# An eleven-tile expert ring, loaded in order, with x kept in HBM between the norms, in a hybrid decoder layer on one core

## What is computed

```python
x = layer_norm(ALPHA * x + g1 * mix, ln1_g, ln1_b)
hf = modulate(x, sh2, sc2)
ff = hier_moe(hf, ...)   # per token: best of 4 groups, then 2 of its 8 experts
#   expert e: (silu(h @ we_gate[e]) * (h @ we_up[e])) @ we_down[e]
x = layer_norm(ALPHA * x + g2 * ff, ln2_g, ln2_b)
```

## Time and profile before

| | us |
|---|---|
| three timed runs | 1441.33, 1443.5, 1445.74 (median 1443.5) |
| the profiled execution | 1444.49 |
| its span, first to last instruction | 1442.7 |
| mixer, up to the last "pb" job | 0 to 669.4 |
| "wo", norms, routing | 669.4 to 797 |
| expert stage on PE | 800.6 to 1373.3 |
| weighing, last norm, stores | 1373.3 to 1442.7 |

### The profile page before, as it was taken

One profiled execution on the slowest core, in us unless ns is written; L12 is line 12 of the kernel. 1 busy time (PEld: TensorE's weight loads), 2 busy tenths in 40 slices (PEclk: granted clock), 3 DMA queues, 4 the chain that ended last, 5 costly groups with the idle time before them and its releaser, 6 DMA issues.

```text
span 1442.7 us, 17957 instructions
## 1 busy us (share of the span) xinstructions
PE 1184.8 (82%) x6154; PEld 722.5 (50%) x6155; DVE 399.3 (28%) x696; ACT 307.8 (21%) x463; POOL 127.2 (9%) x204
## 2 busy tenths in 40 slices
PE   4899999999999999999882687988877888887700
PEld 3687878546778888886442232333323323333200
DVE  3316270143652100103866111111111111111165
ACT  3346470332122000001000021211111111211121
POOL 0100000000000100000000111111111111111134
PEclk9899999899999999999895798999999989999955
DMA  8744431213452314131026559978999999999531
GB/s 282 240 173 160 176 117 59 79 59 120 151 183 88 117 59 175 59 120 33 16 108 256 189 222 400 360 300 329 386 389 401 396 391 369 400 387 370 235 134 46
DMA packets 70232, 307.86 MB, mean 213 GB/s; under 512 B 10079, under 2 KB 18912, under 8 KB 57221
## 3 DMA queue, kind: packets, MB, share of 16 engines
q1 hardware_dynamic: 59946, 295.29, 53.3%
q0 software_dynamic: 6272, 10.14, 2.2%
q10 hardware_dynamic: 3964, 1.73, 0.5%
HBM read 299.00 MB, written 18.55 MB: 220 GB/s over the span
## 4 chain that ended last, share of the span: by engine, by line
PE 63%; DMA 18%; DVE 9%; issue 4%; ACT 3%; SPq 2%; ACTq 0%; POOL 0%; POOLq 0%; DVEq 0%; PEldq 0%
PE ps L1519 29%; DMA mem<-in_we_up 14%; PE ps L1795 13%; PE ps L1804 6%; PE ps L1629 4%; PE ps L1754 3%; PE ps L1787 2%; DMA mem<-in_w_mod 2%; PE ps L1552 1%; DVE mem L1482 1%; DMA mem<-in_we_gate 1%; DVE mem L1481 1%; PE ps L1736 1%; PE ps L1680 1%; DVE mem L1224 1%
## 5 line engine op out<-in xcount | busy, mean ns | idle before, releaser
L1519 PE MATMUL ps<-mem 128*128 128x260 f32 (+1 forms) x2080 | 465.5, 385 | 10.1 <-ACTq L863 3.9
L1519 PEld LDWEIGHTS ps<-mem 128*128 128x128 f32 (+1 forms) x2080 | 391.0, 189 | 80.8 <-issue 12.2
L1795 PE MATMUL ps<-mem 128*64 128x512 f32 x1120 | 287.2, 672 | 94.3 <-DMA mem<-in_we_up 72.6
L1795 PEld LDWEIGHTS ps<-mem 128*64 128x64 f32 x1120 | 90.0, 154 | 265.5 <-issue 265.5
L1461 DVE TENSOR_TENSOR mem<-mem,ps 64x512 f32<-64x512 f32 x35 | 24.1, 690 | 426.7 <-ACT mem L1028 426.7
L1804 PE MATMUL ps<-mem 128*64 128x512 f32 x560 | 129.6, 605 | 3.4 <-issue 3.4
L1028 ACT ACT_TABLE_LOAD x35 | 44.9, 1283 | 367.4 <-PE ps L1795 367.4
L721 POOL DMA_INDIRECT pair_scratch<-mem x35 | 32.7, 934 | 453.9 <-DVE mem L1453 453.9
L1804 PEld LDWEIGHTS ps<-mem 128*64 128x64 f32 x560 | 37.6, 138 | 67.0 <-issue 64.8
L1453 DVE COPY mem<-ps 64x512 f32<-64x512 f32 x70 | 48.2, 688 | 78.4 <-PE ps L1804 77.3
L1754 PE MATMUL ps<-mem 128*128 128x512 f32 x128 | 59.0, 621 | 0.0
(11 more groups left out here) (290 smaller groups left out, 890.5 us busy)
## 6 DMA issues: line engine op xcount, KB each, us to landing
mem<-in_we_gate SPq DMA_DIRECT2D x32, 2048.0 KB, 11.9
mem<-in_we_up SPq DMA_DIRECT2D x32, 2048.0 KB, 15.9
mem<-in_we_down SPq DMA_DIRECT2D x32, 2048.0 KB, 9.0
mem<-in_w_in SPq DMA_DIRECT2D x14, 2048.0 KB, 8.0
mem<-in_w_mod SPq DMA_DIRECT2D x12, 2048.0 KB, 11.6
out<-mem SPq DMA_DIRECT2D x13, 512.0 KB, 5.2
mem<-in_state_gla SPq DMA_DIRECT2D x8, 512.0 KB, 3.9
mem<-v_scratch SPq DMA_DIRECT2D x8, 512.0 KB, 4.2
```

Source lines behind the costliest of these rows:

```text
L1519: ins = pe.matmul(out[0:m, h, 0:HALF], w[:, k, col:col + m], src[:, k, h * HALF:(h + 1) * HALF], start=(k == 0), stop=(k == KD - 1))
L1795: ins = pe.matmul(ps[CAP * q:CAP * q + CAP, 2 + j, :], xT[j][:, k, :], ring[3 * slot + q][:, k, :], start=(k == 0), stop=(k == KD - 1))
```

## The change

The buffers are laid out anew. The six expert tiles become eleven: `gate_ring` and `up_ring` with four slots each, `down_ring` with three. Expert e takes slot e % 4 and e % 3, every expert is loaded in order, and SP's loop is written out for 28 experts. `plan` now gives PE a slot and a turn for each ring; PE picks the slot with nested branches and waits for that slot's semaphore alone.

To make room, x is not held in SBUF: DVE's LN1 loop reads x from three buffers `xb`, loaded from the input again by `load_x`, and SP stores the new x to `x1_scratch` beside `hf` and loads it back as `x1` after the last expert tile. LN1's rows, the modulation and the first three x tiles are loaded during the mixer by SP; LN2's rows and g2 come with `x1` instead of by POOL.

PE's step is written in another order: gate and up of block b, the turn of block b-1's activation, the turn of block b+1's rows, the down product of block b-1. ACT copies the turned activation of b-1 first and takes the silu of b last.

```diff
-            sp.wait_ge(job_done, INDEX[("gb", 7)] + 1)
-            sp.dma_start(mod_samp[0:NS].rearrange("p v d -> p (v d)"), mod_dram[0:NS, 2 * D:5 * D]).then_inc(mod_back, 16)
...
+            def load_x(p):
+                i = ORDER[p]
+                if p >= 3:
+                    sp.wait_ge(x1_out[p % 3], 16)
...
+            for k, name in enumerate(("ln1_g", "ln1_b")):
+                sp.dma_start(lnp[:, k, :], t[name][0:1, :].to_broadcast([P, D])).then_inc(lnp_in, 16)
+            load_x(1)
+            load_x(2)
...
+            def load_gate_up(e):
+                for to, name in ((gate_ring, "we_gate"), (up_ring, "we_up")):
+                    sp.dma_start(to[e % 4], t[name][0, e].rearrange("(p k) n -> p k n", p=P)).then_inc(gu_in[e % 4], 16)
...
+            sp.wait_ge(job_done, INDEX[("gb", 7)] + 1)
+            load_gate_up(0)
+            sp.wait_ge(z_ready, KD)
+            sp.wait_ge(w_used, len(WTILES) - 2)
+            load_down(0)
...
+            sp.wait_ge(rows_out, 64)
+            load_gate_up(1)
+            store_hf(0)
+            store_hf(1)
+            load_x(3)
+            load_x(4)
+            store_hf(2)
+            store_hf(3)
             sp.wait_ge(job_done, INDEX[("wo", ORDER[4])] + 1)
-            load_expert(0, 0, 0)
-            load_expert(0, 1, 0)
-            load_expert(0, 2, 0)
-            load_expert(1, 0, 1)
+            load_down(1)
+            load_gate_up(2)
             store_hf(4)
...
+            load_down(2)
+            load_gate_up(3)
             sp.wait_ge(blocks_ready, 1)
...
+            for e in range(4, NE):
+                after = sp.value_load(plan[0:1, LD_AFTER + e - 4:LD_AFTER + e - 3], min_val=0, max_val=NBLK)
+                sp.wait_ge(gu_done, after + 2)
+                sp.sem_inc(sp_turns, 1)
+                load_gate_up(e)
+                sp.wait_ge(dn_done, after + 2)
+                sp.sem_inc(sp_turns, 1)
+                load_down(e - 1)
...
+            def block_step(i, j):
...
+                    gate_up_of(i * 2 + j, j)
+                    if not first:
+                        turn_act(1 - j, i + (1 + j), i + j)
+                    pe.wait_ge(xg_in[1 - j], i * 16 + 16 * (1 + j))
+                    pe.wait_ge(xT_ready[1 - j], i + (1 + j))
+                    transpose_rows(1 - j)
+                    if not first:
+                        finish(i, j)
```

More of the change, by code:

```diff
@@ L195, in build @@
         K2 = area(Z0 + 2080, HEADS, NT)
+        xn = [area(TB + 1024 * j, D) for j in range(2)]
+        packrows = area(TB + 2048, D)
         EX = area(TB, HEADS, NT)
@@ L311, in build @@
         iota_i = rtmp(64)
[L315 to L325, removed]
+        place_oh = rtmp(2 * TILES, CAP)
+        block_oh = rtmp(2 * TILES, NBLK)
+        named = rtmp(2 * TILES * NBLK * 2).rearrange("p (n b c) -> p n b c", b=NBLK, c=2)
+        assert TB + 3968 >= rt[0] - 2080
         job_done = sem("job_done")
@@ L426, in build @@
         pe_turns = sem("pe_turns")
+        act_turns = sem("act_turns")
         pool_turns = sem("pool_turns")
@@ L740, in _ @@
             two_blocks(0)
-            with pool.Fori(1, NBLK // 2) as i:
+            two_blocks(1)
+            with pool.Fori(2, NBLK // 2) as i:
                 two_blocks(i)
-            for j in range(2):
-                pool.wait_ge(moved[j], 16)
+            pool.wait_ge(tail_in, 16 * 6)
             for p, i in enumerate(ORDER):
@@ new lines, in block_step @@
+            def block_step(i, j):
+                first = isinstance(i, int) and j == 0
+                with sc.If(n > i * 2 + j):
+                    if not first:
+                        copy_acT(1 - j, i + (1 + j), i * 2 + j)
+                    sc.wait_ge(xt_done[1 - j], i + (2 + j))
+                    sc.wait_ge(gu_done, i * 2 + (j + 2))
+                    sc.activation(xT[1 - j], ps[:, 1 - j, :].rearrange("p (k n) -> p k n", k=KD), ACT.Copy)\
+                      .then_inc(xT_ready[1 - j], 1)
+                    sc.wait_ge(gu_done, i * 2 + (j + 3))
+                    sc.wait_ge(act_ready[j], i + 1)
+                    sc.activation(sg[j][CAP:2 * CAP, :], ps[0:CAP, 2 + j, :], ACT.Silu).then_inc(sg_ready[j], 1)
+                if not first:
+                    with sc.Else():
+                        with sc.If(n > i * 2 + (j - 1)):
+                            copy_acT(1 - j, i + (1 + j), i * 2 + j)
+                        sc.sem_inc(act_turns, 1)
@@ L1038, in weigh @@
+            for j in range(2):
+                block_step(0, j)
+            with sc.Fori(1, NBLK // 2) as i:
+                for j in range(2):
+                    block_step(i, j)
             def weigh(i):
@@ L1777, in _ @@
             out = start(("plan", 0))
-            for k in range(5):
+            for k in range(4):
                 ins = pe.matmul(out[0:1, 0, k * NBLK:(k + 1) * NBLK], plan_f[:, k:k + 1], ident[:, 0:NBLK],
@@ L1869 @@
+            for j in range(2):
+                block_step(0, j)
+            with pe.Fori(1, NBLK // 2) as i:
+                for j in range(2):
+                    block_step(i, j)
 _INS = ["x_prompt", "x_sample", "state_conv", "state_rglru", "state_gla", "c_prompt", "c_sample", "w_mod", "b_mod",
```

416 lines of the change are left out of this document (218 added, 198 removed).

## The result

| | us |
|---|---|
| before, median of 4 runs | 1443.01 (1441.33 to 1445.74) |
| changed, median of 4 runs | 1373.41 (1371.09 to 1377.09) |
| ratio | 0.951, interval 0.949 to 0.954 |
| the profiled execution of the changed kernel | 1377.09, span 1375.3 |
| the changed kernel again (experiment 12), median of 5 | 1373.97, ratio 0.953 (0.951 to 0.954) |

The time is 69.6 us lower. The forecast was 1382, with a range of 1365 to 1412: the side and the range held, and the forecast was 8.6 us too high. In the profiled executions PE's last down product ends at 1306.11 where it ended at 1373.33; 1311.6 was forecast. What follows it takes 69.2 us, before 69.4.

The account below looks back on a forecast made before the run. Expert tile transfers were taken to bound the late stage. An earlier start, shorter steps and 16.5 us batches end PE at 1311.6, 61.7 us less, with the tail unchanged: 1444.49 - 61.7 = 1382.8, forecast 1382, range 1365 to 1412.

Parts of the forecast that it names:

- What bounds the stage: Late expert stage bound by expert tile transfer, DMA share 0.97; the stage before leaves the same engines idle, share 0.13.
- The prefetch: Before the first block: eleven expert tiles issued instead of five, 60 us of transfer, ended by some 781, costing nothing.
- The batch: Expert stage: one expert's down, gate and up tiles take 16.5 us; bounds 16.3 and 16.75; twenty batches, 330 us.
- When the queue becomes full: Expert stage: SP's queue idles 10 us before expert 1's end and 7 us before expert 7's, then never empties.
- The step: PE's block step: 12.31 us of products plus 0.2 and 0.7 us of gaps, 13.2 in sum; bounds 12.3 and 14.8.
- The start: Before the expert stage: 4.7 us saved, so the first gate and up product starts at 800.2; bounds 0 and 5.5.
- The working for the first norm's rows: LN1: rows loaded during the mixer let DVE start 3.3 to 3.5 us earlier; 3.5 us counted.
- The last part: From the last gate and up product's start to the last down product's end: 22.8 us, as before the change.
- No shorter step: Rival, chance 0.15: branches and waits keep PE's step at 15.3 us, PE sets the pace, time 1418.
- Fetched again: Rival, chance 0.09 (slower): PE's longer loop is fetched every step, up to 5.7 us each; step 18.9, time 1540.
- Late prefetch: Rival, chance 0.05: waits on SP leave six of eleven tiles, 33 us, for the expert stage; time 1415.

Follow-up runs that it names:

- experiment 12: The changed kernel again, unchanged, as base on the third chip; 1373.97 us, ratio 0.953.
- Experiment 4: Changed kernel loading only half of each expert tile from expert 4 on (down: from expert 3), all engine instructions kept; 1314.07 us.
- experiments 3 and 10: Changed kernel with a smaller ring: 3 has six tiles (two slots of each kind), 1421.22 us; 10 has nine (three slots each), 1387.82 us.
- Experiment 1: Changed kernel with the old order of a block's step on PE and ACT, ring and start kept; 1370.17 us, ratio 0.950.
- experiment 9: Changed kernel with six tiles (two slots each) and the old order of a step on PE and ACT; 1420.96 us, ratio 0.984.
- experiment 7: Changed kernel with the first norm's two rows loaded late again, by ACT's queue behind the last mixer product; 1379.40 us, ratio 0.956.
- experiment 2: Changed kernel with six of the eleven early expert tiles issued only behind the first gathers; 1380.39 us, ratio 0.956.
- experiment 5: Changed kernel with 512 further matrix instructions in PE's block loop, behind a branch never taken; 1373.30 us, ratio 0.952.

## Why the prediction was right, and where its sizes were off

**What bounds the stage: right.** It said that transfers bound the stage, and that the engines stand idle ahead of it while tiles could move. The prefetch came as worked out: the last six tiles are issued from 746.69 and 767.48 (745 and 764 were forecast), and the DMA share from 669 to 790 is 0.51 (near 0.5); only the gate and up of expert 0 came earlier, at 642. Experiment 4 shows the first (60 us gone with half the load), experiments 3 and 10 the second: nine instead of six tiles give 33.4 us, eleven instead of nine 13.9, together 47.2 of the 68. Not all of that is transfer moved ahead. Of the 33.4 us some 14 are the pace, an estimate from 16.65 - 15.96 = 0.69 us for each of the last 20 experts; for the pace the forecast gave depth almost nothing (16.65 to 16.5).

**The batch: right in the mean, wrong in both halves.** 16.5 us were taken for each of the twenty batches behind expert 7. From its end at 954.29, where SP issues the next down tile, to the gate and up product of expert 31 at 1286.31 they take 332.0/20 = 16.6. But this is no constant, and that the mean fits is luck: the forecast let the queue run empty ahead of 958, while at 954 earlier tiles were still queued, and the later batches ran below its bound. The ten batches from 856.42 to 1030.72 take 17.4 us each, and the sixteen experts from there on 15.97. The queues (packets, MB, share of 16 engines' time) from 856 to 1030, then from 1031 to 1286:

```profile
q1 hardware_dynamic: 4427, 64.59, 92.8%
q0 software_dynamic: 2240, 4.27, 7.2%
...
q1 hardware_dynamic: 7271, 102.89, 97.5%
q0 software_dynamic: 2560, 2.78, 3.4%
```

q0 is POOL's gathers and scatters: early they take 7.2% of the engines' time, late 3.4%, since PE's steps of 12.22 us bring them more often and the experts with two blocks have fuller ones (4.27 MB for 14 blocks, 2.78 for 16). What is left to the tiles is 371 GB/s early and 404 late; by the shares 404 would become 404 x 92.8/97.5 = 385, so q0 explains 19 of these 33 GB/s, and the other 14 stay open. And 64.59 MB are 1.7 more than ten batches of 6.29: some tiles issued later had moved before the one that PE waited for had landed.

The forecast had 16.3 us as the least for a batch in a queue that never runs empty, got by scaling a share of 0.97 to 0.99. The measured 15.97 is below it. The scaling holds and the 0.99 does not: the share is 1.01 from 880 to 900 in the kernel before and 1.01 from 860 on in the changed one, and 16.65 x 0.97/1.01 = 15.99. Two rows of the DMA view from 1100 to 1200, GB/s in 40 slices and an expert tile's size and median landing, show where the share was missing. Before:

```profile
GB/s 321 415 442 401 421 419 321 419 423 431 429 426 347 360 429 369 379 433 413 341 334 418 400 438 419 301 367 397 426 365 382 433 295 433 413 418 362 433 347 13
...
mem<-in_we_up SPq DMA_DIRECT2D x6, 2048.0 KB, 16.7
```

And after:

```profile
GB/s 410 390 439 426 426 423 359 382 419 433 439 433 420 338 397 419 433 433 415 446 421 426 426 433 418 393 362 426 419 433 426 439 380 341 439 426 426 410 433 423
...
mem<-in_we_down SPq DMA_DIRECT2D x6, 2048.0 KB, 39.1
```

Before, the last tile of a batch lands 16.7 us after it is issued, and batches are 16.65 us apart: each is issued as the one before runs out, and the rate falls to 350 GB/s or less in nine of the forty slices, to 13 in the last. After, a tile spends 39 us in the queue, with two further batches behind it, and only two slices lie so low. That the pace hangs on the depth is shown by experiments 3 and 10 (16.65 with two slots, 15.96 with three); that it is lost at the handover is read from these rows, and no run took it apart.

**When the queue becomes full: right in kind.** Two idle stretches were forecast, 10 us ahead of expert 1's end and 7 us ahead of that of expert 7. The share of 0.54 from 800 to 860 is the first, and larger; the second did not come, since the share is 1.01 from 860 on, and expert 7 ends at 954.3 where 958.2 was worked out with the longer step.

**The step: forecast 13.2, measured 12.22, and nearly without effect.** The 0.7 us that were left open ahead of the gate and up product are none. One cost was missed, 3.28 us marked issue at 838.75, where PE enters the loop. Experiment 1, with the old order in the same ring, has 0.41 us there, and experiment 3, with the new order and six tiles, none; why is open. The larger miss is one of attribution: the text names the order as what shortens the step, and in experiment 1 the old order has 12.77 us. Its sum gave the step ten times its length's change; between 12.22 and 12.77 that would be 5.5 us, and experiments 1 and 9 show none of it. How long a step may become before the end moves was not tried.

**The start: forecast 800.2, measured 801.62**, and 799.05 in experiment 12. The working for the first norm's rows was 3.5 us; experiment 7 measures 5.4, since in the changed kernel the late loads also meet an expert tile.

**The last part: 22.8 us taken over from before, 19.8 measured.** Its last wait is 1.16 us instead of 2.92, and its last down product 3.67 instead of 5.37; neither the value loads nor PE's clock was counted there. The clock's share is not the change's: the same product takes 5.37 us in experiments 2 and 4. So the 5.5 us by which PE's end was forecast too late are 3.9 of expert 7's earlier end and 3.0 of the last part, less 1.4 of the batches (332.0 us to the last gate and up product where 330.6 were worked out). Of the 8.6 us in all, the other 3 are the profiled execution's distance to the median: 3.7, where 1 was assumed.

**The rivals.** *No shorter step* did not happen. *Fetched again* did not either, by the queue's own rows. *Late prefetch* was priced at 33 us as if each late tile moved the end by its transfer; experiment 2 gives at most 7, because the tiles fall into the empty stretch from 800 to 860. The price belongs to a missing slot, which can't be filled late, not to a late load.

**What stays open.** With six tiles and either order the time is 20 to 21 us below that of the kernel before. Some 6 to 7 us are the start (797.92 and 798.39 against 804.86). The rest lies in the stage (551.6 and 552.3 us in the profiles, against 568.5), and by experiment 9 it is not the order. The shorter gap from two value loads, the experts in list order, and the sixth tile loaded at 743 instead of 803.46 are left; they were not tried one by one.

## What to carry to other kernels

Where a stage is bound by a stream of tiles, count slots, not steps: a slot more moves one tile's transfer out of the stage as long as there is idle queue ahead of it, while a faster consumer gave nothing here, where its step was already below the transfer time of an item. Check whether the landing time of a tile equals the distance between issues; if it does, the queue runs dry at each handover, and one more slot can raise the rate itself, as the third did here and the fourth did not. Before crediting a reordering, run the old order in the new frame: here the ring and the earlier start carried the change and the new order nothing that can be told.

## What was not expected of the hardware

**DVE beside POOL.** In the chain of the changed kernel DVE's pass L1541 takes 1.22 us for the first tile and 3.26 for the second, once POOL's multiply and add have begun; the statistics between them stay at 0.70:

```profile
1318.25 1.22 DVE mem L1541
...
1324.69 3.26 DVE mem L1541
1327.97 0.70 DVE mem L1542
```

The two engines take turns: POOL's multiply that starts at 1331.92 takes 2.34 us and ends at 1334.26, and DVE's pass that starts at 1331.99 ends at 1335.36, 1.10 us behind it. The slow passes read two tensors from SBUF, the statistics one. The Trainium skill, "SBUF — State Buffer", Who interferes with whom, says that a DVE instruction with two SBUF inputs contends with a GpSimd instruction that reads SBUF, and one with a single input does not; the trace agrees.

**An early low clock shows at the end.** Products of the first four blocks take 7.1 us in some executions and up to 9.9 in others (PE's clock from 800 to 860 is 0.97 in experiment 12 and 0.82 in experiment 2), and the whole stage, bound by transfers, is longer by as much: in experiment 5 products at 9.71, 9.89, 6.87 and 8.53 us are 4.6 us more than in experiment 12 (9.31, 7.09, 6.95 and 7.09), and the stage is 505.5 instead of 500.9. In the first profile of the changed kernel they are 1.4 us more and the last gate and up product 1.7 (8.78 instead of 7.09), and the stage has 504.5. It fits experiment 7, where a later start is carried through as well: until the queue is full for good, PE's releases set when it fills. No run sets the clock by itself.
